# Moving joins, the first copies and the first state update ahead of the next pair's work in a pipelined recurrence

## The reference, cut to what matters

```python
def wkv_scan(S0, r, w, k, v, kk, b, reverse):
    def step(S, inp):
        r_t, w_t, k_t, v_t, kk_t, b_t = inp
        sa = -jnp.einsum('bhij,bhj->bhi', S, kk_t)
        S = S * w_t[:, :, None, :] + sa[..., :, None] * b_t[:, :, None, :] + v_t[..., :, None] * k_t[:, :, None, :]
        return S, jnp.einsum('bhij,bhj->bhi', S, r_t)
    xs = tuple(jnp.swapaxes(t, 0, 1) for t in (r, w, k, v, kk, b))
    S, ys = lax.scan(step, S0, xs, reverse=reverse)
    return S, jnp.swapaxes(ys, 0, 1)
...
S0 = jnp.zeros((B, H_A, RWKV_HEAD, RWKV_HEAD), jnp.float32)
for d in range(2):
    S_c, yc = wkv_scan(S0, cx[0], cx[3][:, :, d], cx[4][:, :, d], cx[1], cx[2], cx[5][:, :, d], rev)
    _, yl = wkv_scan(S_c, lat[0], lat[3][:, :, d], lat[4][:, :, d], lat[1], lat[2], lat[5][:, :, d], rev)
```

## Time and profile before

| what | value |
|---|---|
| median of 3 runs | 3934.31 us |
| the profiled execution | 3932.5 us, its span 3930.3 us |
| granted clock in windows of 10 us from 1950 to 2450 us | 1.00 in each |
| PE busy over the span | 3687.3 us (94%) |
| DVE, ACT, POOL busy | 2304.1, 1506.4, 1783.1 us |

### The profile page before, as it was taken

How to read it: one execution, slowest core, us unless ns; L and a number is a source line. 1 busy time by engine, 2 the same in 40 slices (tenths; PEclk the granted TensorE clock), 3 DMA queues, 4 the chain that set the end, 5 groups by cost and what they waited for, 6 DMA issues and landing times. The chain is left out here.

```text
span 3930.3 us, 82342 instructions
## 1 busy us (share of the span) xinstructions
PE 3687.3 (94%) x33759; PEld 3218.6 (82%) x33759; DVE 2304.1 (59%) x4366; ACT 1506.4 (38%) x2831; POOL 1783.1 (45%) x1218
## 2 busy tenths in 40 slices
PE   8989899999898999989899999889999899988997
PEld 6867799999676888778788888679999777668996
DVE  4354566666553776675577775276666630737665
ACT  3244433333365443342244443243333231744443
POOL 0201555554343877532244332165555232737884
PEclk9999999999999999989999999999999999989998
DMA  5132233332201444332211100233333121012331
GB/s 190 60 121 93 96 118 108 108 108 91 71 6 57 159 156 161 124 115 109 79 26 29 26 22 24 91 102 108 108 108 108 65 85 48 21 60 70 108 98 64
DMA packets 159987, 343.85 MB, mean 87 GB/s; under 512 B 33535, under 2 KB 89343, under 8 KB 159359
## 3 DMA queue, kind: packets, MB, share of 16 engines
q1 hardware_dynamic: 139743, 266.23, 20.4%
q10 hardware_dynamic: 19872, 72.36, 5.4%
HBM read 323.74 MB, written 16.93 MB: 87 GB/s over the span
## 5 line engine op out<-in xcount | busy, mean ns | idle before, releaser
L1351 POOL TENSOR_TENSOR feed_low<-feed_sums,feed_high 128x512 fp32r<-128x512 f32 x320 | 502.5, 1589 | 466.7 <-ACT feed_high L1345 458.6
L1351 POOL TENSOR_TENSOR feed_low<-ring,feed_high 128x512 fp32r<-128x512 f32 x448 | 594.6, 1343 | 193.8 <-ACT feed_high L1345 96.7
L1345 ACT ACTIVATE feed_high<-ring 128x512 fp32r<-128x512 f32 x448 | 278.9, 626 | 432.2 <-PE ps L1596 243.0
L1580 PE MATMUL ps<-hn_high,feed_high 128*128 128x384 f32 (+1 forms) x1280 | 401.8, 314 | 0.2 <-POOL feed_low L1351 0.2
L1581 PE MATMUL ps<-hn_low,feed_high 128*128 128x384 f32 (+1 forms) x1280 | 395.4, 309 | 0.0
L1582 PE MATMUL ps<-hn_high,feed_low 128*128 128x384 f32 (+1 forms) x1280 | 395.3, 309 | 0.0
L1594 PE MATMUL ps<-feed_hid,feed_high 128*128 128x384 f32 (+1 forms) x1056 | 379.7, 360 | 13.0 <-DVE h L1778 5.5
L1595 PE MATMUL ps<-feed_hid,feed_high 128*128 128x384 f32 (+1 forms) x1056 | 376.9, 357 | 0.0
L1596 PE MATMUL ps<-feed_hid,feed_low 128*128 128x384 f32 (+1 forms) x1056 | 376.7, 357 | 0.0
L1345 ACT ACTIVATE feed_high<-feed_sums 128x512 fp32r<-128x512 f32 x320 | 189.7, 626 | 487.7 <-DVE feed_sums L1370 344.6
L1580 PE MATMUL ps<-cross_high,feed_high 128*128 128x384 f32 (+1 forms) x960 | 297.8, 310 | 6.5 <-issue 5.7
(11 more groups left out here) (647 smaller groups left out, 9472.4 us busy)
## 6 DMA issues: line engine op xcount, KB each, us to landing
feed_side_ring<-in_ada ACTq DMA_DIRECT2D x138, 512.0 KB, 4.4
ring<-in_ffn_g SPq DMA_DIRECT2D x88, 512.0 KB, 5.0
ring<-in_ffn_u SPq DMA_DIRECT2D x88, 512.0 KB, 3.8
ring<-in_ffn_d SPq DMA_DIRECT2D x88, 512.0 KB, 3.8
diff_side_ring<-in_ada SPq DMA_DIRECT2D x32, 512.0 KB, 4.3
ring<-in_od_in SPq DMA_DIRECT2D x24, 512.0 KB, 4.1
ring<-in_ev_in SPq DMA_DIRECT2D x23, 512.0 KB, 5.2
ring<-in_even_in SPq DMA_DIRECT2D x20, 512.0 KB, 4.4
```

The costliest lines, as they stand in the source:

```text
L1345: act.activation(self.high[:, e % self.SLOTS, :], self.source(name, n), ACT.Copy).then_inc(self.high_ready, 1)
L1351: pool.tensor_tensor(self.low[:, slot, :], self.source(name, n), self.high[:, slot, :].bitcast(F32), ALU.subtract).then_inc(self.low_ready, 1)
L1580: pe.matmul(dst, high, vh, start=c == 0, stop=False)
```

## The change

All edits are in `rwkv_pairs`, and none is to what is computed:
- PE: four fill products are put behind `gate(e)` in level 2, with a wait on `a_ready` in rounds with a next pair; the five at the end of the join become two.
- PE, DVE: step 0 has no products with the state, which is zero, no wait for it, no `memset` and no `sf`; the first state update adds a tile of zeros.
- PE: at s = 2 `turn_unit(j, 0)` and `triangle_unit(j, 0)` move from the middle to the end of the step.
- ACT: the 0.5x + 0.5 of the rate (`halve_rate`) is split off `linear_rate` and, for d = 1, moves ahead of the joins; `exponentials(j, 1)` moves from ahead of step 0 to behind its copies; `copy_values(j, 0)` moves from the end of step 0 to the middle of step 1.
- DVE: `gate_y` moves ahead of level 4; `join(i, 0)` moves ahead of `centre(j, 1)`, which stands between the two joins now; `receptance(j, 1)` moves from step 0 to step 1.

The diff (twelve leading blanks of each line are left out):

```diff
--- before.py
+++ after.py
@@ -3576,6 +3576,10 @@
             u_products(i, l, 1)
         if reading and l == 2:
             gate(e)
+            if inverting:
+                if preparing:
+                    pe.wait_ge(S["a_ready"], 2 * j + 1)
+                unread(6, 4)
         if alone:
             unread(4, 2 if l == 2 else 1)
         if inverting:
@@ -3592,7 +3596,7 @@
             join_second(i, c)
             if c == 1:
                 unread(6, 1)
-        unread(6, 5)
@@ -3660,16 +3664,19 @@
             v_ = [vt[:, i % 2, n, :] for n in ns]
             q_ = [qq[:, i % 2, d, n, :, :] for d, n in enumerate(ns)]
             for d in range(2):
-                pe.wait_ge(S["state_ready"], 24 * i + (2 * s + d + 1))
+                if s > 0:
+                    pe.wait_ge(S["state_ready"], 22 * i + (2 * (s - 1) + d + 1))
                 for hs in HALVES:
-                    pe.matmul(Z[d][hs, :], q_[d][hs, 0, :], state[d][hs, :], start=True, stop=False)
-                    mm = pe.matmul(Z[d][hs, :], lt[d][hs, s, 2, :], v_[d][hs, :], start=False, stop=True)
+                    if s > 0:
+                        pe.matmul(Z[d][hs, :], q_[d][hs, 0, :], state[d][hs, :], start=True, stop=False)
+                    mm = pe.matmul(Z[d][hs, :], lt[d][hs, s, 2, :], v_[d][hs, :], start=s == 0, stop=True)
                 mm.then_inc(S["z_done"], 1)
             for d in range(2):
                 for hs in HALVES:
-                    pe.matmul(yc[d][hs, :], state[d][hs, :], q_[d][hs, 1, :], start=False, stop=False)
+                    if s > 0:
+                        pe.matmul(yc[d][hs, :], state[d][hs, :], q_[d][hs, 1, :], start=False, stop=False)
                     pe.matmul(yc[d][hs, :], v_[d][hs, :], lt[d][hs, s, 3, :], start=False, stop=False)
-        if j < PAIRS and s >= 2:
+        if j < PAIRS and (s > 2 or s == 2 and i < 0):
             turn_unit(j, s - 2)
         if i >= 0:
             for d in range(2):
@@ -3695,6 +3702,9 @@
             for d in range(2):
                 for hs in HALVES:
                     mm = pe.matmul(yc[d][hs, :], sa[hs, d, :], lt[d][hs, s, 1, :], start=False, stop=d == 1 and s in (3, 11))
+        if j < PAIRS and s == 2 and i >= 0:
+            turn_unit(j, 0)
+            triangle_unit(j, 0)
     if i >= 0:
         mm.then_inc(S["y_done"], 1)
     if j < PAIRS:
@@ -3739,9 +3749,11 @@
         act.wait_ge(S["op_done"], q)
     act.activation(a, R3, ACT.Tanh, scale=0.5, bias=half_bias(j, 2 + d)).then_inc(S["a_ready"], 1)
 
-def linear_rate(j, d):
+def halve_rate():
     act.drain()
     act.activation(a, a, ACT.Copy, scale=0.5, bias=0.5)
+
+def linear_rate(j, d):
     act.wait_ge(S["cum_ready"], 2 * j + d + 1)
     act.drain()
     act.activation(decay, chunked(a), ACT.Identity, scale=p(j, "k_a"), bias=complement[:, j:j + 1]).then_inc(S["lin_ready"], 1)
@@ -3807,6 +3819,7 @@
         copy_g(i, 2, 0)
         copy_g(i, 2, 1)
     if preparing:
+        halve_rate()
         linear_rate(j, 0)
     if inverting:
         copy_g(i, 2, 2)
@@ -3828,11 +3841,15 @@
     if inverting:
         for c in range(4):
             copy_join(i, c)
+    if preparing:
+        halve_rate()
+    if inverting:
         join(i, 1)
         join(i, 3)
     if preparing:
         linear_rate(j, 1)
-        exponentials(j, 1)
+        if not inverting:
+            exponentials(j, 1)
 
 def copy_values(j, part):
     act.wait_ge(S["v_turned"], 2 * j + part + 1)
@@ -3852,10 +3869,14 @@
             for d in range(2):
                 act.wait_ge(S["z_done"], 24 * i + (2 * s + d + 1))
                 act.activation(zs[:, d, :], k.ps[:, d, 0:64], ACT.Copy).then_inc(S["z_copied"], 1)
+            if j < PAIRS and s == 1:
+                copy_values(j, 0)
             for d in range(2):
                 act.wait_ge(S["sa_done"], 24 * i + (2 * s + d + 1))
                 act.activation(sa[:, d, :], k.ps[:, d, 64:128], ACT.Copy, scale=-1.0).then_inc(S["sa_copied"], 1)
-        if j < PAIRS and s < 2:
+        if j < PAIRS and s == 0 and i >= 0:
+            exponentials(j, 1)
+        if j < PAIRS and s < 2 and (s == 1 or i < 0):
             copy_values(j, s)
         if j < PAIRS and s >= 2:
             copy_turned(j, s - 2)
@@ -3999,19 +4020,18 @@
             inverse(i, 3, c)
     if preparing:
         updates(j, 0)
+    if reading:
+        gate_y(e)
     if inverting:
         for c in range(4):
             inverse(i, 4, c)
     if preparing:
         scan(j, 1)
+    if inverting:
+        join(i, 0)
+    if preparing:
         centre(j, 1)
     if inverting:
-        for d in range(2):
-            dve.memset(sm[:, d, 0, :], 0.0).then_inc(S["state_ready"], 1)
-    if reading:
-        gate_y(e)
-    if inverting:
-        join(i, 0)
         join(i, 2)
     if preparing and not inverting:
         finish(j, 0)
@@ -4021,8 +4041,8 @@
 def finish(j, part):
     if part == 0:
         query(j, 1)
+    if part == 1:
         receptance(j, 1)
-    if part == 1:
         updates(j, 1)
     if part == 2:
         key_sums(j)
@@ -4040,12 +4060,14 @@
         if i >= 0 and s < NCH - 1:
             f = [factor[:, i % 2, d, ORDER[d][s]:ORDER[d][s] + 1] for d in range(2)]
             dve.drain()
+            if s > 0:
+                for d in range(2):
+                    dve.tensor_scalar(sf[:, d, :], sm[:, d, s % 2, :], f[d], None, ALU.mult)
+                dve.drain()
             for d in range(2):
-                dve.tensor_scalar(sf[:, d, :], sm[:, d, s % 2, :], f[d], None, ALU.mult)
-            dve.drain()
-            for d in range(2):
+                kept = sf[:, d, :] if s > 0 else zeros[:, 0:HEAD]
                 dve.wait_ge(S["ds_done"], 22 * i + (2 * s + d + 1))
-                dve.scalar_tensor_tensor(out=sm[:, d, (s + 1) % 2, :], in0=k.ps[:, 2 + d, 0:64], scalar=f[d], in1=sf[:, d, :],
+                dve.scalar_tensor_tensor(out=sm[:, d, (s + 1) % 2, :], in0=k.ps[:, 2 + d, 0:64], scalar=f[d], in1=kept,
                                          op0=ALU.mult, op1=ALU.add).then_inc(S["state_ready"], 1)
         if j < PAIRS and i >= 0 and s < 3:
             finish(j, s)
```

More of the change, by code:

```diff
@@ L3594, in advance @@
                             unread(6, 1)
-                    unread(6, 5)
+                    unread(6, 2)
             def turn_values(j, part):
```

## The result

The changed kernel took 3917.89 us (median of 7, 3912.04 to 3921.40), the kernel before, beside it, 3935.45 (7 executions, 3932.25 to 3953.31). The ratio is 0.9946, 95% interval 0.9927 to 0.9965. The forecast was 3924.8: its sign was right and its gain of 9.5 us little more than half of the 17.6 between the medians. The ratio, which weighs all executions and not the medians alone, stands for 21 us, more than twice the forecast. The profiled executions took 3932.5 and 3914.18, spans 3930.3 and 3912.4.

The account below looks back on a forecast made before the run. TensorE was taken to bound the recurrence, with a few holes. First turn 2.25, turns 2 to 5 4 x 1.8 = 7.2, last 0: 9.45 us off the profiled 3932.5 gives 3923.0, plus 1.8 is 3924.8 us; range 3917 to 3937.

Parts of the forecast that it names:

- TensorE bounds the stage and the hole of step 0 pays: Recurrence stage: TensorE busy 82.68 of 86.90 us; closing step 0's 1.24 us hole starts `zs` 2.2 us earlier.
- Step 1's `zs` isn't held up by the exponentials: Step 1 on ScalarE: exponentials end at 2172.4, `zs` copy wanted at 2172.55; they just fit.
- the second rival: Turn: nothing left, moved exponentials or VectorE's `finish` cost 1.8 us a turn; 3934; 0.17 together with another rival.
- VectorE's update in step 2 is late next: Step 2 on VectorE: added `receptance`, some 0.9 us, leaves 1.8 of the 2.2 us won.
- `query` beside GpSimd: VectorE's `query` overlapping GpSimd's multiply: 0.33 us at half speed, no delay; as a lock 0.2 a turn, 3925.8 us.
- The fills: Level 2, four products behind the gate: 1.0 us into a 0.75 hole, 0.25 a turn; 1.0 in the last round.
- The clock at the turns: Turns: granted clock stays 1.00; rival that it falls in steps 0 and 1, losing 22 us, 3947, chance 0.07.
- the sum: Whole stage: 2.25 first turn, 7.2 turns 2 to 5, 0 last round; 9.45 us, other work the same.

Follow-up runs that it names:

- ScalarE's order alone: Kernel before with only the ScalarE edits: halving ahead of the joins, exponentials behind step 0's copies, values copied in step 1; 3940.12 us, ratio 1.0014.
- The third run of after: The changed kernel, unchanged, run again on the same chip as two others of its call; 3917.67 us, beside 3940.95 for the kernel before.
- the two filled ones: Kernel before with five more fill products in step 0's hole in each turn preparing a pair, run twice; 3930.28 us (ratio 0.9983) and 3932.23 us (0.9997).

## Why the forecast was right, and where it was too small

- **TensorE bounds the stage and the hole of step 0 pays.** Right in what pays: same TensorE work, period 86.9 to 84.9 or 85.1 (forecast 85.1). It is too simple as a whole: fills at the gate cost nothing because TensorE waits for VectorE's join at the turn, and from the first state update to the triangle of step 3 VectorE's work sets the time. The exponentials' move is shown as the main part (1.6 a turn), `gate_y` 0.6, the zero state 0.2. They don't simply add up: ScalarE's order alone gave 0.6 to 1.0, for it brought step 0's `sf` beside GpSimd, a wait that no part of the forecast has.
- **Step 1's `zs` isn't held up by the exponentials.** Right; the second rival fell.
- **VectorE's update in step 2 is late next.** Right, with 0.22 us at step 3. The advance was 2.2 at step 0 in the forecast, 1.8 after step 2, and 1.95 was measured.
- **`query` beside GpSimd.** Priced at half speed. The size was wrong: it behaved nearer the lock, by which the forecast would have been 3925.8, further from the measurement; it was covered all the same.
- **The fills.** Priced at 0.25 a turn and 1.0 in the last round. The first is 0.0; the second no run shows, as traces of one kernel differ by 1.4 us there.
- **The clock at the turns.** Right for this kernel: 1.00 in the turn's window. It is no empty rival: it fell there in several relatives.

The step that failed is the sum, in what it leaves at nothing. It holds 2.25 + 7.2 + 0 = 9.45 us for the stage and 0 for all the rest. The stage gave 11.8 in the same traces: 7.7 in the four repeated periods, 0.8 in the last round where I took 0, and 3.3 up to the first update. The 0.8 isn't safe: the last round took 81.28 and 82.24 us in the two traces of before and 80.52, 81.12 and 81.95 in the three of after. The 3.3 has two parts. From the first turn's scan to the first update were 9.55 us and are 6.97, 2.6 less; 0.4 of it is lost again until step 4. The timelines of after:

```profile
1986.58 1.78 DVE L3902 TENSOR_TENSOR_SCAN ring<-rwkv_within,ring 128x780 f32<-128x780 f32 x1
```

```profile
1991.77 0.45 PE L3685 MATMUL ps<-rwkv_zs,rwkv_xd 64*64 64x64 f32 x8 [0.21 <-ACT rwkv_zs L3871]
...
2004.95 0.34 PE L3671 MATMUL ps<-rwkv_sm,rwkv_qq 64*64 64x64 f32 x4
```

From scan to step 4 are 18.37 us, 2.15 less than the 20.52 before (1990.48 to 2011.00); 2.25 were forecast, so the turn itself is the forecast's. The other 0.7 lies ahead of that scan, where the granted clock over 81 us was 0.96, and 0.91 in the kernel before. It goes with the clock and not with the edit. The third run of after and the kernel before with its hole filled have it the other way round:

```profile
1908.46:1989.46 81.00, 75.09 (x1299) 64.21 (x1300) 54.71 (x87) 33.54 (x57) 37.56 (x29) 0.91 0.24 66
1909.27:1990.27 81.00, 72.83 (x1328) 62.28 (x1329) 55.32 (x88) 33.53 (x57) 37.54 (x29) 0.96 0.24 66
```

From the stage's first instruction to the first turn's scan were 82.9 us in the first, an after, and 82.2 in the second, a before; the pair above has 82.3 and 83.0.

The larger miss is what the sum puts at nothing: 6.1 of the profiled 17.9 us of span lie outside the stage. The forecast carried everything there over unchanged, and had a changed clock only as a risk on the slow side. It also carried over that the median lies 1.8 us above the profiled execution; in after it lies 3.7 above. Over all traces, the parts outside sum to 3367.5 to 3374.3 us in the six kernels built on before (mean 3370.5) and 3361.8 to 3372.2 in the eleven built on after (mean 3366.4). Behind the stage the two groups don't overlap: 1461.9 to 1462.7 us in the four of them whose hole isn't filled, 1456.2 to 1461.4 in the thirteen other traces, the two filled ones among them. The gap between the groups is only 0.5 us, for `gate_y` put back has the 1461.4; the other twelve end at 1459.3. One place where it arises, 100 us of nearly the same work in before:

```profile
3500.00:3550.00 50.00, 39.75 (x284) 32.53 (x283) 28.29 (x52) 22.99 (x39) 22.99 (x16) 0.80 0.16 53
3550.00:3600.00 50.00, 40.53 (x278) 37.87 (x276) 37.42 (x52) 21.52 (x38) 38.26 (x26) 0.90 0.20 64
```

and in after:

```profile
3484.80:3534.80 50.00, 38.95 (x288) 31.49 (x287) 28.96 (x51) 22.62 (x39) 23.49 (x17) 0.86 0.17 53
3534.80:3584.80 50.00, 39.73 (x281) 37.17 (x280) 38.93 (x53) 23.27 (x41) 40.69 (x27) 0.97 0.20 64
```

The granted clock is 0.80 and 0.90 in the one, 0.86 and 0.97 in the other. That is as far as the rows go. Why a stage that is over a thousand microseconds back should matter isn't settled, and the cause of these 6.1 us stays open. That holes in it do this was only argued: the two filled kernels speak for it, the one with the exponentials put back (hole 1.84 us, 1458.5 behind the stage) against it. Part of the outside difference may be chance between executions.

There is one more sign of the same kind. The three runs of after spread over 9.4 us in 20 executions (3912.0 to 3921.4), and the kernel before over 42 in 99 (3924.9 to 3967.4), a quarter of them above 3945. Its median thus holds time that no single quiet trace shows.

## What to carry to other kernels

Follow a chain over the whole hand-over: the move that pays (here two exponentials out from between two products) pays in full only when what stands in front on the other engines, `gate_y` here, goes too. A part of the change tried alone can bring two engines beside each other that the whole keeps apart, as `sf` and GpSimd here. An edit that closes TensorE's holes came here with more time than the holes' length, and one that shifted fills away from a hole lost more; read the granted clock ahead of, in and behind the edited stage, compare traces that were granted the same, and set the clock on both sides of the range. Compare spreads as well as medians.

## What the runs showed of the hardware

- The low clock can last long under full load: 34.1 us at 0.50 with TensorE busy all the time, 2.8 us behind a hole of 0.74 us, for about 13 us of lost time. In the other traces the stretches between the first and the last turn were of 3.4 or 6.8 us, and those of 3.4 cost 1.0 and 1.6 us where they stand alone (85.93 against 84.9; 86.76 against 85.1).
- A VectorE multiply of 128x768 that started 0.82 us before GpSimd's ended took 1.63 us, against 0.95 alone: it lost all of the overlap but 0.14 us. Two VectorE `sf` instructions of 128x64 that began beside GpSimd's multiplies took 3.10 us, against 0.42 alone, and ended when GpSimd did.
- Five products of 128x512 put into a hole of 1.24 us moved nothing behind them.
